# The preceding item's down product ahead of the last gate and up chunk, in items of 64 rows

## The reference, cut to what matters

```python
gu = xb @ w_gate_up[e] + b_gate_up[e]      # 1024 -> 2048
g, u = gu[:, :D_FF_EXPERT], gu[:, D_FF_EXPERT:]
g = jnp.minimum(g, SWIGLU_LIMIT)
u = jnp.clip(u, -SWIGLU_LIMIT, SWIGLU_LIMIT)
a = (u + 1.0) * (g * jax.nn.sigmoid(SWIGLU_ALPHA * g))
return a @ w_down[e] + b_down[e]           # 1024 -> 1024
```

## Time and profile before

| | us |
|---|---|
| median of 3 runs | 1426.43 |
| lowest, highest | 1424.15, 1429.24 |
| profiled execution | 1425.06 |
| its span, first to last instruction | 1423.3 |

### The profile page before, as it was taken

The page is one execution under the profiler, slowest core; times in us unless marked ns, Lnnn a source line. Parts: engine busy times, 40 slices in busy tenths (PEclk is TensorE's granted clock), DMA queues, the critical chain, the costliest instruction groups (busy, mean ns, idle before and its releaser), DMA issues.

```text
span 1423.3 us, 27518 instructions
## 1 busy us (share of the span) xinstructions
PE 1368.0 (96%) x11227; PEld 648.5 (46%) x11227; DVE 742.6 (52%) x1481; ACT 224.5 (16%) x417; POOL 190.7 (13%) x242
## 2 busy tenths in 40 slices
PE   6999999999999999999999999999999999999999
PEld 5888887778953333323232323323232232323234
DVE  5213736765257475444745544564644446465543
ACT  5224436642220000000000000000000000000000
POOL 2001400000002112020211202021120202112020
PEclk9999999999999999999999999999999999999999
DMA  6332320003689999999999999999999999999994
GB/s 193 91 116 70 108 89 1 2 31 115 255 304 364 408 402 414 401 411 413 412 410 400 421 409 410 413 411 417 402 421 400 414 410 414 412 410 413 396 412 175
DMA packets 59704, 447.28 MB, mean 314 GB/s; under 512 B 8656, under 2 KB 26096, under 8 KB 35056
## 3 DMA queue, kind: packets, MB, share of 16 engines
q1 hardware_dynamic: 56528, 436.22, 76.8%
q0 software_dynamic: 3072, 10.49, 2.3%
q10 hardware_dynamic: 64, 0.02, 0.0%
HBM read 442.51 MB, written 4.19 MB: 314 GB/s over the span
## 4 chain that ended last, share of the span: by engine, by line
PE 75%; DMA 19%; issue 4%; ACT 1%; DVE 1%; POOL 0%; SPq 0%; POOLq 0%; ACTq 0%; DVEq 0%
PE ps L1881 31%; DMA gu_head<-in_w_gate_up_dram 11%; PE ps L1916 9%; DMA gu_tail<-in_w_gate_up_dram 7%; PE ps L1848 7%; PE ps L1518 3%; PE ps L1519 3%; PE ps L1520 3%; PE ps L1924 2%; PE ps L1542 2%; PE ps L1540 2%; PE ps L1541 2%; PE ps L1509 1%; PE ps L1511 1%; PE ps L1510 1%
## 5 line engine op out<-in xcount | busy, mean ns | idle before, releaser
L1881 PE MATMUL ps<-gu_head,xT 128*32 128x512 f32 x2304 | 257.2, 594 | 2.7 <-DMA gu_head<-in_w_gate_up_dram 2.7
L1347 DVE TENSOR_TENSOR x_tok<-x_tok,ps 128x1024 f32<-128x1024 f32 x60 | 73.3, 1222 | 249.8 <-PE ps L1848 249.8
L1881 PE MATMUL ps<-gu_head,xT_odd 128*32 128x512 f32 x1536 | 169.1, 593 | 0.9 <-DVE act_gu L1311 0.6
L918 ACT ACTIVATE act_s<-act_gu 128x768 f32<-128x768 f32 (+1 forms) x32 | 23.6, 738 | 922.0 <-DVE act_gu L1322 922.0
L1881 PEld LDWEIGHTS ps<-gu_head,xT 128*32 128x32 f32 x2304 | 70.7, 110 | 169.2 <-issue 156.8
L1311 DVE STREAM_TRANSPOSE act_gu<-ps 128x512 f32<-128x512 f32 x80 | 57.3, 716 | 140.5 <-PE ps L1881 135.5
L695 POOL DMA_INDIRECT xg<-h_dram,idx_g x32 | 70.0, 2186 | 438.4 <-DVE row_all L1280 438.4
L1916 PE MATMUL ps<-dn_even,aT 128*32 128x512 f32 x1024 | 116.1, 594 | 0.0
L958 DVE TENSOR_TENSOR st_l<-st_w,st_h 128x2048 fp32r<-128x2048 f32 x25 | 57.3, 2292 | 109.4 <-ACT st_h L759 109.4
L1916 PE MATMUL ps<-dn_odd,aT 128*32 128x512 f32 x960 | 106.1, 594 | 0.0
L1881 PEld LDWEIGHTS ps<-gu_head,xT_odd 128*32 128x32 f32 x1536 | 49.3, 110 | 116.9 <-issue 111.3
(11 more groups left out here) (402 smaller groups left out, 2038.1 us busy)
## 6 DMA issues: line engine op xcount, KB each, us to landing
gu_head<-in_w_gate_up_dram SPq DMA_DIRECT2D x96, 2048.0 KB, 23.9
gu_tail<-in_w_gate_up_dram SPq DMA_DIRECT2D x32, 2048.0 KB, 20.5
dn_even<-in_w_down_dram SPq DMA_DIRECT2D x32, 2048.0 KB, 25.3
dn_odd<-in_w_down_dram SPq DMA_DIRECT2D x32, 2048.0 KB, 21.4
st_w<-in_w_in_dram SPq DMA_DIRECT2D x17, 1024.0 KB, 5.3
st_w<-in_w_out_dram SPq DMA_DIRECT2D x4, 1024.0 KB, 5.1
x_tok<-in_x_dram SPq DMA_DIRECT2D x4, 512.0 KB, 5.0
st_w<-in_w_o_swa_dram SPq DMA_DIRECT2D x4, 512.0 KB, 3.5
```

The costliest lines, as they stand in the source:

```text
L1347: v.tensor_tensor(x_tok[:, c, :].rearrange("p (h n) -> p h n", h=2), x_tok[:, c, :].rearrange("p (h n) -> p h n", h=2), ps[:, SUM_BANKS, : ...
L1881: ins = pe.matmul(ps[j * GROUP:(j + 1) * GROUP, n, :], rows_of(i)[:, k, n * GROUP:(n + 1) * GROUP], gu_columns(k, j), start=(k == 0), stop ...
```

## The change: what it does

- In an odd item the loop's `down(0, pair)` is issued by TensorE after k step 5 of `gate_up(1, pair)`, that is ahead of chunk 3, and no longer after `lists(3)`. In even items `down(1)` stays behind `lists(4)`.
- The last item takes the same form: its `down(0)` moves from after k step 3 to after k step 5.
- VectorE: in an odd item `turn_rows(2)` comes first, then `keep_low(0)`, then `turn_out(1)`. In an even item the order stays as it was.
- ScalarE: the round is now `weigh(0)`, `sigmoid(1)`, `sigmoid(2)`, `weigh(1)`.
- SP's and GpSimd's programs are the same.

```diff
             with act.Fori(0, n_pairs) as pair:
-                for i in (1, 2):
-                    sigmoid(i, pair)
-                    weigh(i - 1, pair)
+                weigh(0, pair)
+                sigmoid(1, pair)
+                sigmoid(2, pair)
+                weigh(1, pair)
...
-                    turn_out(i, pair)
-                    turn_rows(i + 1, pair)
+                    if i == 1:
+                        turn_rows(2, pair)
+                        keep_low(0, pair)
+                        turn_out(1, pair)
+                    else:
+                        turn_out(2, pair)
+                        turn_rows(3, pair)
                     index(i + 2, pair)
                     keep_gates(i + 2, pair)
                     activate(i, e, pair)
-                    keep_low(i - 1, pair)
+                    if i == 2:
+                        keep_low(1, pair)
...
-            def gate_up(i, pair=None, last=False):
+            def gate_up(i, pair=None):
...
-                    if last and k == 3:
+                    if i == 1 and k == 5:
                         down(0, pair)
...
                 for i in (1, 2):
                     gate_up(i, pair)
                     lists(i + 2, pair)
-                    down(i - 1, pair)
-            gate_up(1, n_pairs, last=True)
+                    if i == 2:
+                        down(1, pair)
+            gate_up(1, n_pairs)
```

## The result

| | before | changed |
|---|---|---|
| median of 22 runs each, us | 1426.59 | 1429.54 |
| lowest to highest | 1423.7 to 1430.09 | 1426.6 to 1434.87 |
| profiled execution (span) | 1425.06 (1423.3) | 1429.01 (1427.1) |
| granted clock, mean | 0.991 | 0.988 |

The ratio, taken between runs made side by side, is 1.0017, with a 95% interval from 1.0009 to 1.0024: 2.4 us more (1.3 to 3.4), inside the 0.3% that was called no change. The two medians of the table lie 2.95 us apart. The forecast was 2.0 us more, a median of 1428.4.

The account below looks back on a forecast made before the run. The prediction took the full stream of weights, 62.94 us a round, as the bound. First-round hole 0.7, last item 0.5 and clock 0.8 summed to +2.0 us, a median of 1428.4 us, range 1422.5 to 1438.

Parts of the forecast that it names:

- The stream bounds the rounds, the wait is moved, not removed: Loop rounds: weights take 62.94 us a round, so TensorE's wait goes from chunk 3 to the next item's first chunk, 0 us of gain.
- Copying out exposed by 1.0 us: Before gate_up(2): TensorE waits about 1.0 us a round for turn_out(1), hidden by the wait for weights.
- Turn_rows at nothing: VectorE: turn_rows(2) ahead of copying out is the same work earlier, done before TensorE is through chunk 3; 0 us.
- The hole in the first round, 0.7 us (0 to 2.5): First round: SP's later request for a weight chunk lets the stream run dry once, shifting all later landings by 0.7 us.
- The hole by that estimate: First round: about 1.5 us if all of the 2 us fixed DMA cost lay ahead of the data.
- The last item, +0.5: Last item: down(0) behind chunk 2 waits 0.2 us, last activation and down product 0.3 us late; range 0 to 1.5.
- 82 to 84 us that were named as a sign: Span from the landing of item 30's first weight chunk to the end, expected in the profile after.
- The clock, +0.8 as one chance in two of 1.7: At item 30's first weight chunk: a 2.7 us wait may halve TensorE's clock, costing 1.7 us; ends 0 and 1.7.
- TensorE becomes the bound: Loop rounds: copying out and two clock falls make 63.6 us a round; +8 us, 1434 us, chance 0.08.

## Why the prediction was right, step by step

- *The stream bounds the rounds, the wait is moved, not removed.* Right. The waits on chunks were 30.2 us, 27.5 of them for gu_tail, and are 29.8 us for gu_head. Over the 13 rounds from item 4 to item 30, e0's landing moves by 818.8 us in the changed kernel, 62.98 a round (forecast 62.94). With the stream made faster, the changed kernel waits for no chunk at all, and its waits and time came out as for a kernel that TensorE bounds.
- *Copying out exposed by 1.0 us.* Right, 0.84 us, and its cover is what was named.
- *Turn_rows at nothing.* Right: TensorE waits for it nowhere in the changed kernel. With VectorE's old order the change costs 90 us.
- *The hole in the first round, 0.7 us (0 to 2.5).* The mechanism, the place (request at 469.1, measured 469.21) and "once only" were right. The size was not: 2.4 to 2.6 us, at the upper end. The sum took the landing of e2 as the time at which the engines run out of data. But e2, asked for at 455.48, landed at 469.7 in the changed kernel, while the share was down to 0.18 from 467.6 on: most of the engines had run out some 2 us before the landing. To that comes the 0.94 us from request to data, which had been bounded rightly by 1.
- *By the Trainium skill's "DMA: Bandwidth & Descriptors", section "Anatomy of one DMA — SWDGE (gpsimd) path",* a DMA's fixed cost is about 2 us. The hole by that estimate was 1.5 us. That section is on DMAs issued by GpSimd, while these are issued by SyncE, and it puts most of the 2 us behind the last byte, not ahead of the first. The trace has 0.94 us from request to data, and about 1 us from the last data that the rows show (468.7) to the landing at 469.7. The 2.4 to 2.6 us are not such a fixed cost: their larger part is engines that ran out one after another from 467 us on, which neither estimate counted.
- *The last item, +0.5.* Measured 81.9 against 81.7 us, +0.2, just under the 82 to 84 us that were named as a sign.
- *The clock, +0.8 as one chance in two of 1.7.* In the profiled execution of the changed kernel the wait for e0 of item 30 was 1.12 us and the clock didn't fall there. In the one with the first round old it did, for 1.3 us. In the changed kernel's second profile the wait was 3.30 us and it didn't fall. What share of executions pays this can't be read from a few traces. Nor were the waits 2.7 us each: they go from 1.1 to 3.8 us. In three rounds of the changed kernel the clock was down for 6.8 us, as long as the two falls of the rival *TensorE becomes the bound*, and the first two k steps took 8.11 for 5.36 us:

```profile
1280.86:1287.68 6.82, 5.60 (x28) 1.38 (x32) 4.31 (x10) 0.63 (x1) 1.53 (x1) 0.50 1.02 400
1282.08 8.11 PE ps L1888 x48
```

It was hidden even so, and the wait after it was only 1.12 us: what the prediction held against that rival, that longer slowed work makes the next wait shorter, is what happened.
- *By "TensorE: Matmul & The Clock Gate", section "HAM oscillation — how this bites in real kernels", of the Trainium skill* waits in a loop could throttle each round. With waits of 6.97 us they did so in every round, and it cost 2.1 us of each. In the changed kernel, with waits of 1.1 to 3.8 us, the falls came in every second round, and the stream hid them.

The forecast of +2.0 was a sum of one term too small by about 1.8 us and two too large, by 0.3 and, in the profiled execution, 0.8. So the forecast's nearness to the measured 2.4 us is in part luck: errors of opposite sign. Of the 3.6 us by which e0 of item 30 came late in the profiled execution, 2.7 were there at e0 of item 4 (526.4 against 523.7 us). The other 0.9 us lie in the rate of the stream: from e0 of item 4 to that of item 30 the 13 rounds took 817.0 to 821.6 us in the traces of the kernels with full gathers and an unbroken stream. That spread is as large as the effect, so a single pair of traces could not have given it.

## What to carry to other kernels

Where a stream of loads is full on both sides of a wait, ask of a new order not what it takes off the waiting engine but when it frees the buffers, and look at the first round by itself: there the loads have no lead yet, and the time from when the engines run out until the late request's data come is lost for good. A landing time is the end of the slowest part of a transfer; count the reserve from the time when the engines fall idle, some 2 us earlier here. And where the orders of two engines were changed together, undoing one of them alone cost more than either version did, twice here.

## What the runs showed of the hardware that was not expected

- Two gathers of 64 and 96 rows of 4 KB beside the weights cost more than their bytes. Cut to 16 rows each (0.52 MB less, 1.2 us at 428 GB/s) the round of the stream fell from 62.9 to 60.1 us (e0 of item 4 at 519.8, of item 30 at 1300.9 us), by 2.8 us.
- The length of a wait didn't settle how long the granted clock fell, or whether it fell. It was 0.50 for 6.8 us at the wait of 4.33 us and at waits of 6.97 us, but also at waits of 3.57, 3.76 and 3.82 us in the changed kernel. It was 0.50 for 3.4 us after a wait of 4.09 us in that kernel's second profile, and stayed at 1.00 after one of 3.30 us there.
